# Seven block products for 8 of 22 activation tiles in three of the four down projections of an FP32 encoder kernel

## What is computed

```python
def swiglu(h, w_gate, w_up, w_down):
    return (jax.nn.silu(h @ w_gate) * (h @ w_up)) @ w_down
# D_MODEL = 1024, D_FF = 2816, SEQ = 512
h = h + 0.5 * swiglu(rms_norm(h, norms[i, 0]), ffn_w_gate[i, 0], ffn_w_up[i, 0], ffn_w_down[i, 0])
```

## Time and profile before

| | |
|---|---|
| median of 3 runs | 1891.66 us (1890.3 to 1891.82) |
| the profiled execution | 1889.01 us, of which 1887.2 us are the span from first to last instruction |
| mean granted clock of TensorE | 0.998 of full speed |
| PE busy | 1858.4 us, 98% |
| DVE, ACT, POOL busy | 1354.8, 895.7, 260.9 us |

### The profile page before, as it was taken

The page is one execution under the profiler, slowest core; times in us unless marked ns, Lnnn a source line. Parts: engine busy times, 40 slices in busy tenths (PEclk is TensorE's granted clock), DMA queues, the critical chain, the costliest instruction groups (busy, mean ns, idle before and its releaser), DMA issues.

```text
span 1887.2 us, 31448 instructions
## 1 busy us (share of the span) xinstructions
PE 1858.4 (98%) x11418; PEld 1615.1 (86%) x11418; DVE 1354.8 (72%) x1983; ACT 895.7 (47%) x1509; POOL 260.9 (14%) x204
## 2 busy tenths in 40 slices
PE   8999999999999999999999999999989999999998
PEld 6899988777799998887899998877658899998886
DVE  8788788774988874357888864269984988874355
ACT  7455542245555563234455553244563655554222
POOL 0000001312100000234000001073243100000225
PEclk9999999999999999999999999999999999999999
DMA  5233333332233333323333332232101233333321
GB/s 180 90 112 101 99 106 105 96 100 86 78 98 95 109 112 111 111 67 101 100 92 99 111 123 96 93 109 68 57 1 46 91 100 99 111 105 118 105 74 56
DMA packets 56753, 179.88 MB, mean 95 GB/s; under 512 B 12144, under 2 KB 12144, under 8 KB 56656
## 3 DMA queue, kind: packets, MB, share of 16 engines
q1 hardware_dynamic: 54656, 173.69, 29.7%
q0 software_dynamic: 928, 3.02, 0.5%
q10 hardware_dynamic: 1088, 2.10, 0.3%
HBM read 175.04 MB, written 3.15 MB: 94 GB/s over the span
## 4 chain that ended last, share of the span: by engine, by line
PE 87%; DVE 9%; ACT 2%; POOL 1%; issue 1%; DMA 0%; DVEq 0%; SPq 0%; POOLq 0%; ACTq 0%
PE ps L2314 36%; PE ps L2276 26%; PE ps L2258 17%; PE ps L2762 2%; PE ps L2425 1%; DVE work L1256 1%; DVE sm L1280 1%; DVE stat L1254 1%; POOL sumsq L1556 1%; DVE x_lo L441 1%; ACT prob L1998 0%; PE ps L2476 0%; PE ps L2288 0%; DVE sm L1299 0%; PE ps L2711 0%
## 5 line engine op out<-in xcount | busy, mean ns | idle before, releaser
L389 DVE TENSOR_TENSOR w_lo<-raw,w_hi 128x1024 fp32r<-128x1024 f32 x174 | 231.6, 1340 | 217.0 <-ACT w_hi L381 216.3
L381 ACT ACTIVATE w_hi<-raw 128x1024 fp32r<-128x1024 f32 x186 | 194.2, 1054 | 293.9 <-PE ps L2276 248.7
L2314 PE MATMUL ps<-xs_hi,w_hi 128*128 128x256 f32 x1088 | 308.2, 283 | 0.5
L2314 PE MATMUL ps<-xs_lo,w_hi 128*128 128x256 f32 x1088 | 307.9, 283 | 0.0
L2314 PE MATMUL ps<-xs_hi,w_lo 128*128 128x256 f32 x1088 | 307.9, 283 | 0.0
L2276 PE MATMUL ps<-act_hi,w_hi 128*128 (+1 forms) x720 | 280.5, 390 | 0.0
L2276 PE MATMUL ps<-act_lo,w_hi 128*128 (+1 forms) x720 | 280.1, 389 | 0.0
L2276 PE MATMUL ps<-act_hi,w_lo 128*128 (+1 forms) x720 | 280.1, 389 | 0.0
L2258 PE MATMUL ps<-x_hi,w_hi 128*128 128x512 f32 x640 | 257.5, 402 | 8.5 <-ACT w_hi L381 7.2
L2258 PE MATMUL ps<-x_hi,w_lo 128*128 128x512 f32 x640 | 250.2, 391 | 0.0
L2258 PE MATMUL ps<-x_lo,w_hi 128*128 128x512 f32 x640 | 249.8, 390 | 0.0
(11 more groups left out here) (412 smaller groups left out, 3545.5 us busy)
## 6 DMA issues: line engine op xcount, KB each, us to landing
raw<-in_weights SPq DMA_DIRECT2D x322, 512.0 KB, 3.6
h<-in_xT ACTq DMA_DIRECT2D x4, 512.0 KB, 6.4
out<-result SPq DMA_DIRECT2D x4, 512.0 KB, 3.0
p_raw<-in_pT POOLq DMA_DIRECT2D x2, 512.0 KB, 4.2
scratch_u<-u_sc SPq DMA_DIRECT2D x1, 512.0 KB, 6.6
u_grp<-scratch_u SPq DMA_DIRECT2D x1, 512.0 KB, 4.1
scratch_y<-y_grp SPq DMA_DIRECT2D x2, 256.0 KB, 3.1
y_ch<-scratch_y SPq DMA_DIRECT2D x1, 512.0 KB, 3.6
```

Source lines behind the costliest of these rows:

```text
L381: act.activation(w_hi[:, slot], raw[:, slot], ACT.Copy).then_inc(hi_ready, 1)
L389: dve.tensor_tensor(w_lo[:, slot], raw[:, slot], w_hi[:, slot].bitcast(F32), SUB)\
L2314: last = pe.matmul(ps[:, bank, 0:HALF], w[:, at, cols], x[:, k], start=(start and k == 0 and part == 0), stop=(stop and k == KH - 1 and pa ...
```

## The change

In the second, third and fourth down projection (f = 1, 2, 3; `MIXED_DOWN`) activation tiles 0 to 7 leave the two groups. Each group keeps tiles 8 to 21: 7 chunks instead of 11. Between the groups stand four "mixed" tiles c = 0 to 3. A mixed tile computes the contribution of activation tiles 0 to 7 to the two output tiles 2c and 2c+1 in seven block products of 12 matmuls on 256 tokens, where plain products take 48 matmuls on 512 tokens. The four sums of activation blocks (`block_sum`) are made by DVE during the last up tiles, and split by ACT and DVE during group 0 (`block_hi`, `block_lo`). The splits of tiles 0 and 1 leave `last_tile`. A mixed tile's two places of `raw` are each loaded by two DMAs of 256 KB with runs of 512 bytes, since its weight tiles come from four chunks. Its results are added to `h` by DVE in six parts (`added`). SP's and DVE's loops around it are written out. In the diff below, `last_tile` is DVE's; ACT's drops `act_high` of tiles 0 and 1 in the same way. The last two lines are POOL's, ahead of the sum of squares. The first down projection stays as it was.

```diff
+MIXED_DOWN = (1, 2, 3)
+ACTS_BEFORE = tuple(sum(NF - KD * (g in MIXED_DOWN) for g in range(f)) for f in range(4))
+DOWN_STEPS = (NF - KD) // 2
+DOWN_MIXED = DOWN_STEPS
+DOWN_LAST = DOWN_STEPS + KD
...
+            def block_sum(o):
+                upper, lower = acts[:, 0:KH], acts[:, KH:KD]
+                right, left = slice(HALF, T), slice(0, HALF)
+                if o == 0:
+                    dve.wait_ge(s["prod_done"], KD + NF * f)
+                    ins = dve.tensor_tensor(b_sum[0][:], lower[:, :, right], upper[:, :, right], SUB)
...
             def last_tile(i, b):
-                act_low(dve, f, 0)
-                act_low(dve, f, 1)
+                if f in MIXED_DOWN:
+                    block_sum(3)
+                else:
+                    act_low(dve, f, 0)
+                    act_low(dve, f, 1)
...
+            fast_tile(NF // 2 - 2, 0)
+            if f in MIXED_DOWN:
+                block_sum(0)
+            fast_tile(NF // 2 - 2, 1)
+            if f in MIXED_DOWN:
+                block_sum(2)
             fast_tile(NF // 2 - 1, 0)
+            if f in MIXED_DOWN:
+                block_sum(1)
             last_tile(NF // 2 - 1, 1)
...
+        def mixed_down_dve(dve, n, first, q, after=None):
...
+            def weight_sums(c):
+                b11, b21, b12, b22 = mixed_raw(start, c)
...
+                dve.tensor_tensor(w_sum[:, 0], b11, b12, ADD).then_inc(mixed["w_sums"], 1)
+                dve.tensor_tensor(w_sum[:, 1], b22, b12, ADD).then_inc(mixed["w_sums"], 1)
+                dve.wait_ge(mixed["w_sums"], 4 * g + 1)
+                dve.tensor_tensor(w_sum[:, 2], w_sum[:, 0], b22, ADD).then_inc(mixed["w_sums"], 1)
+                dve.wait_ge(mixed["w_sums"], 4 * g + 3)
+                dve.tensor_tensor(w_sum[:, 3], w_sum[:, 2], b21, ADD).then_inc(mixed["w_sums"], 1)
...
+            for j in range(DOWN_STEPS):
+                if AHEAD + j < DOWN_STEPS:
+                    split_lo(dve, first, AHEAD + j)
+                act_low(dve, f, KD + 2 * j)
+                act_low(dve, f, KD + 2 * j + 1)
+                if j in (1, 2):
+                    block_lo(2 * j - 2)
+                    block_lo(2 * j - 1)
...
+                if j == 5:
+                    weight_sums(0)
+                    own_lo(0, 0)
+            sum_lo(0, "T13", 1)
+            sum_lo(0, "T2", 2)
+            sum_lo(0, "T4", 3)
+            for k in range(GROUP - 1):
+                update(k, mixed["h_part"])
+            own_lo(0, 1)
+            update(GROUP - 1, mixed["h_part"])
...
+            for c in range(GROUP):
+                more = c + 1 < GROUP
+                if more:
+                    weight_sums(c + 1)
+                added(c, 0)
+                if more:
+                    sum_lo(c + 1, "T4", 1)
+                    sum_lo(c + 1, "T2", 2)
+                added(c, 1)
+                if more:
+                    own_lo(c + 1, 0)
+                else:
+                    split_lo(dve, first, DOWN_LAST)
+                added(c, 2)
+                added(c, 3)
+                if more:
+                    sum_lo(c + 1, "T13", 3)
+                    own_lo(c + 1, 1)
+                else:
+                    split_lo(dve, first, DOWN_LAST + 1)
+                added(c, 4)
+                added(c, 5)
...
+            def load_down(first):
+                for j in range(NF):
+                    place = first + j
+                    if DOWN_MIXED <= j < DOWN_LAST:
...
+                        sp.wait_ge(split_ready, place - SLOTS + 1)
+                        for row in range(2):
+                            sp.dma_start(raw[:, place % SLOTS, row::2],
+                                         A["weights"][begin:begin + KH, :, d + GROUP * row]
+                                         .rearrange("c p f -> p c f"))\
+                              .then_inc(raw_loaded[place % SLOTS], 16)
...
+        def mixed_down_act(act, n, first, after=None):
...
+            for j in range(DOWN_STEPS):
+                if AHEAD + j < DOWN_STEPS:
+                    split_hi(act, first, AHEAD + j)
+                act_high(act, f, KD + 2 * j, first)
+                act_high(act, f, KD + 2 * j + 1, first)
+                if j in (0, 1):
+                    block_hi(2 * j)
+                    block_hi(2 * j + 1)
...
+            for c in range(GROUP):
+                more = c + 1 < GROUP
+                copied(c, 0)
+                copied(c, 1)
+                copied(c, 2)
+                if more:
+                    sum_hi(c + 1, "T4")
+                    sum_hi(c + 1, "T2")
+                    own_hi(c + 1, 0)
...
+                copied(c, 3)
+                if more:
+                    sum_hi(c + 1, "T13")
+                    own_hi(c + 1, 1)
...
+            def mixed_tile(c):
...
+                pe.wait_ge(split_ready, start + 2 * c + 1)
...
+                product(first_bank, at["B11"], parts[4], True, False, mixed["product"])
+                pe.wait_ge(mixed["t_ready"], 3 * g + (3 if c else 1))
+                product(right_bank, at["T1"], parts[0], True, False, mixed["product"])
+                pe.wait_ge(mixed["t_ready"], 3 * g + 3)
+                pe.wait_ge(mixed["copied"], 4 * g + 1)
+                product(first_bank, at["T2"], parts[1], False, False, mixed["product"])
+                product(left_bank, at["B21"], parts[5], True, True, mixed["product"])
+                pe.wait_ge(mixed["copied"], 4 * g + 3)
+                product(first_bank, at["T3"], parts[2], False, False, mixed["product"])
+                pe.wait_ge(split_ready, start + 2 * c + 2)
+                product(right_bank, at["B22"], parts[3], False, True, chunk_used)
+                pe.wait_ge(mixed["copied"], 4 * g + 4)
+                product(first_bank, at["T4"], parts[6], False, True, chunk_used)
+
+            for m in range(DOWN_STEPS):
+                ready(pe, m)
+                down_chunk(pe, first, m, 0, m == 0, m == DOWN_STEPS - 1,
+                           static(act_hi, m), static(act_lo, m))
+            for c in range(GROUP):
+                mixed_tile(c)
...
+            def ready(pe, m):
+                pe.wait_ge(ffn_sems["act_ready"], m * 2 + 2 + ACTS_BEFORE[f])
...
+                    if FFN_OF.get(n) in MIXED_DOWN:
+                        pool.wait_ge(chunk_used, DOWN_STARTS[FFN_OF[n]] + DOWN_LAST)
```

More of the change, by code:

```diff
@@ L334, in encoder @@
             "t_ready", "product", "copied")}
+        mixed = {n: sem(f"mixed_{n}") for n in (
+            "sums", "b_hi", "b_ready", "w_sums", "t_hi", "t_ready", "product", "copied", "added",
+            "late", "h_part")}
         tab = sem("tab")
@@ L371, in turn_of, with loads_of @@
             return i + (first + j) // SLOTS
+        def loads_of(first, j, i=0):
+            twice = sum(first + j >= DOWN_STARTS[f] + DOWN_LAST for f in MIXED_DOWN)
+            return i * 16 + (turn_of(first, j) * 16 + 16 + 32 * twice)
         def split_hi(act, first, j, i=0):
@@ L1810, in last_tile @@
             def last_tile(i, b):
-                act_high(act, f, 0)
-                act_high(act, f, 1)
+                if f not in MIXED_DOWN:
+                    act_high(act, f, 0)
+                    act_high(act, f, 1)
                 copy_part(i, b, 0)
@@ L2399, in down_pe, with mixed_down_pe, static, product @@
                     m += 1
+        def mixed_down_pe(pe, f, n, first, ready):
+            u = MIXED_BEFORE[f]
+            start = first + DOWN_MIXED
+            def static(a, m):
+                at = KD + 2 * m
+                return lambda row: a[:, (at + row) * T:(at + row + 1) * T]
+            def product(bank, at, x, begin, end_, done):
+                for k in range(KH):
+                    cols = slice(k * P, (k + 1) * P)
+                    for part, (w, rhs) in enumerate(((wf_hi, x[0]), (wf_hi, x[1]), (wf_lo, x[0]))):
+                        last = pe.matmul(ps[:, bank, 0:HALF], w[:, at, cols], rhs[:, k],
+                                         start=(begin and k == 0 and part == 0),
+                                         stop=(end_ and k == KH - 1 and part == 2),
+                                         skip_group_check=True)
+                last.then_inc(done, 1)
+            def mixed_tile(c):
+                g = 4 * u + c
+                at = mixed_halves(start, c)
+                first_bank, left_bank, right_bank = mixed_banks(c)
+                parts = [(b_hi[o], b_lo[o]) for o in range(4)]
+                for rows, cols in ((slice(0, KH), slice(0, HALF)), (slice(KH, KD), slice(0, HALF)),
+                                   (slice(KH, KD), slice(HALF, T))):
+                    parts.append((acts_hi[:, rows, cols], acts_lo[:, rows, cols]))
+                pe.wait_ge(split_ready, start + 2 * c + 1)
+                if c == 0:
+                    pe.wait_ge(mixed["b_ready"], 7 * (u + 1))
+                if c == 1:
+                    pe.wait_ge(mixed["h_part"], GROUP * (u + 1))
```

(8 more changed lines are left out.)

271 lines of the change are left out of this document (247 added, 24 removed).

## The result

| | before | after |
|---|---|---|
| median of 5 runs | 1891.66 us (1890.3 to 1891.87) | 1899.82 us (1898.71 to 1903.53) |
| profiled execution | 1889.01 us | 1898.71 us |
| mean granted clock in it | 0.998 | 0.995 |

The ratio of the changed kernel to the one before is 1.0053, with a 95% interval of 1.0042 to 1.0064. That is 10.0 us of 1891.66 (7.9 to 12.1); the two medians are 8.2 us apart. The change makes the kernel slower, by half a per cent. The five executions fall into two groups, 1898.7 to 1899.8 and 1903.5 us (two of them); only one of the first group was profiled, so that where the other 4 us lie is not shown.

The account below looks back on a forecast made before the run. The prediction took PE's issue as the bound and summed -9.4 (saving) + 12.5 (waits) + 2.9 (clock) = +6.0 us: 1895.0 us for the profiled execution, 1897.7 us for the median, range 1893.8 to 1901.0 us.

Parts of the forecast that it names:

- The saving: Three changed down projections: 336 short matmuls for 192 long ones save 3.12 us each, 9.4 us in all.
- The start: Before chunk 0 of each changed projection: PE waits 4.05 us for tiles 8 and 9, 4.15 with restart, 12.5 for three.
- The clock: Behind the waits at the projections' starts: the granted clock falls to half, costing 2.9 us in all.
- I take it behind two of three waits: Starts of the changed projections: the clock falls after two of three waits, 1.45 us each, 2.9 us.
- 1.7 us lost if all of it lies on matmuls: Behind a wait: a low-clock stretch of 3.4 us holds half the matmuls, losing between 1.2 and 1.7 us.
- each time in full, 5.1 us: Upper bound of the clock's loss: a full fall behind every one of the three waits, 5.1 us.
- The mixed tiles: Between the two groups: PE needs 10.1 us a tile and waits for nothing, taken as 0; bound +9 us.
- DVE has the last operand 1.0 us before PE wants it: Mixed tiles: DVE finishes the last operand for product 2 of the next tile 1.0 us before PE needs it.
- What is late next? Nothing: Chunk 1, behind the starting wait: tiles 10 and 11, wanted at 713.2, are done near 710.4 (ACT) and 712 (DVE).
- Loads, block sums, splits in group 0, POOL: Around the changed projections: these edits are hidden and cost nothing; uncovered block sums would cost 3 us a projection.
- the clock holds: Rival at the projections' starts: three waits of 4.15 us without a fall, +3.1 us, 1894.8 us; chance 0.16.
- the wait is not there: Rival before chunk 0: no wait, saving stands alone, 1882.3 us; a wait under 3.1 us decides; chance 0.10.

Follow-up runs that it names:

- kernel 2: Changed kernel with activation tiles 8 and 9 split before PE's last up product and the block splits one chunk later: 1882.9 us, ratio 0.9957 to the kernel before.
- kernel 4: Changed kernel with four unused FP32 matmuls put in PE's wait before chunk 0: 1895.24 us, ratio 1.0021 to the kernel before.
- kernel 1: Changed kernel with activation tiles 8 and 9 split before PE's last up product: 1892.05 us, ratio 1.0009 to the kernel before.
- kernel 8: Changed kernel with tiles 8 and 9 split ahead of the weight chunk, run twice: 1893.51 and 1895.11 us, ratios 1.0016 and 1.0017 to the kernel before.
- kernel 6: The changed kernel run again, nothing altered: 1899.41 us, ratio 1.0051 to the kernel before.
- kernel 5: Kernel before, without mixed tiles, with tiles 0 and 1 split after the last up tile in three down projections: 1909.36 us, ratio 1.0102 to the kernel before.
- kernel 7: Changed kernel with two block splits of ACT moved ahead of the high parts of tiles 8 and 9: 1904.29 us, ratio 1.0068 to the kernel before.

## What the prediction had right, and the step that failed

The direction and the mechanism came out as forecast: waits of about 4 us, a fall of the clock behind them, and nothing lost in the mixed tiles. The step that failed is the size of one term of the sum, the clock: 2.9 us stood there and 5.6 were measured. This is 2.7 of the 3.7 us that lie between the 6.0 of the sum and the 9.7 of the profiled execution (10.0 by the ratio); the other 1.1 us passed ahead of the three changed projections.

- **The saving** was put at 3.12 us each, measured 3.18 (kernel 2, 119.71 against 116.53).
- **The start** was walked through row by row to 4.05 us, with both engines' order; the chain shows 3.93 from end to start, 4.09 by starts, and kernel 4 gives 4.2 with the restart for the predicted 4.15. The forecast of the sign rests on this term, and it held: three waits cost 12.5 us in kernel 4, and 12.5 stood in the sum.
- **The clock** is where the sum fell short. The step was "I take it behind two of three waits", at 1.45 each, 2.9 us. Measured are 2.7 + 1.3 + 1.6 = 5.6 us in the profiled execution. Two things were off. The count: it fell behind each of nine waits of 3.93 us. And the size of one: "1.7 us lost if all of it lies on matmuls" took the one fall of the earlier trace rows, 3.4 us long, as the longest there is, but behind one of the three waits the clock was low for 6.8 us. So the bound "each time in full, 5.1 us" was itself too low. One fall in a trace tells that a fall is possible; it is no bound of its length. Nor did that one fall show a price: in the profile after, PE has the same idle time of 2.01 us in the mixer (before 1381.45) and the clock stays up, yet the stretch between the third and the fourth projection takes 467.05 us, as it did before (467.02). The Trainium skill ("TensorE: Matmul & The Clock Gate", "Why this matters for your kernels"), by which a fall would come behind every gap of this size, was the better guide for the count; the runs agree for 3.93 us. The page has gaps over about 3 us; here gaps of 2.2 and 2.52 us brought a fall in some cases too (experiments 1 and 8), and by the measurement those count as well. The one fall of the earlier trace rows stood behind 2.01 us, so it bore out a fall but not that size. By the rule the forecast would have been 1.5 us higher, and still short by the second stretch.
- **The mixed tiles** were put at no wait of their own: right, 40.31 us for 336 matmuls each time. "DVE has the last operand 1.0 us before PE wants it" was 0.9: the low part is done at 779.30 + 1.22 = 780.52, PE's product begins at 781.42. DVE's wait for ACT, put at about 1 us a tile, was 0.74 to 0.79.

```profile
779.30 1.22 DVE L874 TENSOR_TENSOR w_lo<-w_sum,w_hi 128x1024 fp32r<-128x1024 f32 x1
...
781.42 0.28 PE L2772 MATMUL ps<-b_hi,w_hi 128*128 128x256 f32 x1
```

- **"What is late next? Nothing"** was right for the changed kernel, but its cover was the very wait: take that away and chunk 1 is 2.2 us late (kernel 1). The prediction named ACT's and DVE's work before tiles 10 and 11 and its time, but not that it would be later than PE if PE were not held up.
- **Loads, block sums, splits in group 0, POOL** at nothing: right. The loads of 256 KB landed in 3.2 us, and the chain has no other new piece.

The sum by terms: -9.5 for -9.4, +12.5 for +12.5, +5.6 for +2.9, and 1.1 us ahead of the three changed projections, which no term had. That gives 9.7 us for the predicted 6.0. The median of 1899.82 us lies inside the range, but the ratio times 1891.66, 1901.7 us, lies above its end of 1901.0. The range reached 1 us beyond three short falls in full; with one long one, and the 1 us from elsewhere, there was no room left. Of the rivals, "the clock holds" is answered by kernels 4 and 6, "the wait is not there" by the chain. Had the wait been under 3.1 us, that rival said, the change would gain; kernel 8 is such a case (2.52 us of idle time, 2.7 by starts) and is 0.16% slower. Even without a fall its wait costs 3.1 us, since group 0 behind it takes 0.4 us longer as well, and with a fall 1.25 us more. So with this order the point that decides is at about 2.7 us, not 3.1, and the clock has to stay up too.

Open is why one stretch lasts 3.4 and another 6.8 us behind the same wait. The changed kernel and kernels 5 and 6 show both, kernel 7 with its longer wait only the long one, kernel 8 only the short one, and no run here tells what decides it.

## What to carry to other kernels

Where PE sets the time with dense matmuls, a stall of 4 to 5 us cost itself and then 1.3 to 2.9 us for the clock, in all twelve cases profiled here; one of 2.5 us cost 1.25 us for it in one execution and nothing in another. Count both, and take the higher figure for the bound. When tiles are taken out of the front of a chain, the ones that become first need the early preparation that the old first ones had, and whatever has no hurry (block splits for 38 us later) belongs behind what the next chunk wants. A wait that hides other lateness must be removed together with it: the early split alone gained 7.8 us on the changed kernel, with the block splits moved too it gained 16.9 (by the medians). What a few unused matmuls in the stall are worth is shown by experiment 4: they gave back the clock's part, not the wait's. And an engine's idle time is margin only if it does not wait for something that itself waits for that engine.

## What the runs showed of the hardware

The clock fell behind two of three waits of 2.2 us (experiment 1), behind none of three of 2.52 us in one execution and all three in another (experiment 8), and behind all twelve of 3.93 and 5.20 us. The low level lasted 3.4 us in five of these twelve and 6.8 in seven, although PE was at dense matmuls of 512 tokens again for up to 6.2 us of it. On such matmuls it costs 47% of the stretch (one start every 0.427 us, for 0.227). It can begin after PE has restarted: 0.84 us after in the third projection of the changed kernel. With PE idle for only 0.45 of the 4 us it did not fall (experiment 4).

The thin matmuls of the second layer's mixer see such falls as well, without any change there. In kernel 2 (windows, granted clock third from the end):

```profile
1371.20:1377.90 6.70, 5.78 (x21) 3.85 (x22) 5.75 (x20) 2.88 (x11) 1.51 (x4) 0.50 0.00 0
1402.00:1405.00 3.00, 3.00 (x16) 2.14 (x16) 2.96 (x9) 2.48 (x6) 1.61 (x2) 0.50 0.00 0
```

There, where PE often waits for others, a fall need not cost anything. The stretch between the third and the fourth down projection, which holds this mixer, took 467.02 us before with 3.4 us at the low level, 467.05 in the changed kernel with none, and 467.05 and 467.11 in kernels 5 and 6 with 6.8 us each. In kernel 2 it took 471.18 us, with 13.7 us at the low level in three stretches, one of them (3.4 us from 1258.5) on matmuls of 512 tokens. So a stretch of low clock can cost nothing in one place (the mixer) and nearly half its length in another (the start of the down projections).

How much of the difference between executions of one kernel this explains is only in part shown. Of the runs of the kernel before beside these experiments, those with a mean clock of 0.998 or 0.999 took 1889.2 to 1890.4 us and those with 0.996 took 1891.2 to 1892.0; but those with 0.997, half of all, took anything from 1889.7 to 1892.5.
